# Two feed-forward layers: six interleaved stages a layer instead of three passes, 24 groups of seven products instead of 16

## What is computed

```python
def swiglu(h, w_gate, w_up, w_down):
    return (jax.nn.silu(h @ w_gate) * (h @ w_up)) @ w_down

def reference(x, positions, ...):
    cos, sin = rope_tables(positions)
    for l in range(DEPTH):                       # DEPTH = 2
        if l < N_A:                              # layer 0
            x = x + multiscale_pool_mixer(rms_norm(x, pool_norm[l]), ...)
        else:                                    # layer 1
            x = x + mla_layer_mixer(rms_norm(x, attn_norm[b]), ..., cos, sin)
        x = x + swiglu(rms_norm(x, ffn_norm[l]), w_gate[l], w_up[l], w_down[l])
    return rms_norm(x, final_norm)
```

## Time and profile before

| what | value |
|---|---|
| median of three runs | 1746.03 us |
| the three runs | 1746.16, 1745.45, 1746.03 us |
| the profiled execution | 1746.25 us, its span 1744.4 us |
| PE, DVE, ACT, POOL busy | 1736.1, 1339.1, 986.0, 168.2 us |
| granted PE clock | 1.0 in all slices |
| read from HBM | 326.01 MB |

### The profile page before, as it was taken

One profiled execution on the slowest core, in us unless ns is written; L12 is line 12 of the kernel. 1 busy time (PEld: TensorE's weight loads), 2 busy tenths in 40 slices (PEclk: granted clock), 3 DMA queues, 4 the chain that ended last, 5 costly groups with the idle time before them and its releaser, 6 DMA issues. The chain is left out here.

```text
span 1744.4 us, 29460 instructions
## 1 busy us (share of the span) xinstructions
PE 1736.1 (100%) x11142; PEld 1575.2 (90%) x11142; DVE 1339.1 (77%) x1772; ACT 986.0 (57%) x1336; POOL 168.2 (10%) x196
## 2 busy tenths in 40 slices
PE   9999999999999999999999999999999999999998
PEld 6899988999889999889999888998899998899987
DVE  5898766788667886788997779876678866788665
ACT  6666543566435665466775456664356653466543
POOL 2100000000000000324112420000000000000000
PEclk9999999999999999999999999999999999999999
DMA  6678665786767876665445457867568866688762
GB/s 227 216 231 245 234 192 190 238 252 170 248 200 203 251 232 216 200 199 159 150 139 170 156 165 244 242 186 252 196 191 246 247 214 203 200 252 243 227 214 91
DMA packets 103937, 363.24 MB, mean 208 GB/s; under 512 B 11664, under 2 KB 13072, under 8 KB 103696
## 3 DMA queue, kind: packets, MB, share of 16 engines
q1 hardware_dynamic: 94320, 327.03, 54.5%
q0 software_dynamic: 9216, 33.56, 11.2%
q10 hardware_dynamic: 288, 1.11, 0.2%
HBM read 326.01 MB, written 2.10 MB: 188 GB/s over the span
## 5 line engine op out<-in xcount | busy, mean ns | idle before, releaser
L1594 DVE TENSOR_TENSOR w_lo<-raw,w_hi 128x1024 fp32r<-128x1024 f32 (+1 forms) x720 | 858.0, 1201 | 257.3 <-ACT w_hi L1148 251.4
L1148 ACT ACTIVATE w_hi<-raw 128x1024 fp32r<-128x1024 f32 (+1 forms) x721 | 741.4, 1035 | 473.9 <-PE ps L635 390.2
L634 PE MATMUL ps<-xg,w_hi 128*128 128x512 f32 x1856 | 653.2, 392 | 0.8 <-DVE w_lo L1594 0.3
L635 PE MATMUL ps<-xg,w_lo 128*128 128x256 f32 x1856 | 522.9, 282 | 0.0
L634 PE MATMUL ps<-act,w_hi 128*128 128x512 f32 x1352 | 469.2, 390 | 0.0
L634 PEld LDWEIGHTS ps<-xg,w_hi 128*128 128x128 f32 x1856 | 348.4, 188 | 72.2 <-DVE w_lo L1594 2.3
L635 PE MATMUL ps<-act,w_lo 128*128 128x256 f32 x1352 | 381.2, 282 | 0.0
L635 PEld LDWEIGHTS ps<-xg,w_lo 128*128 128x128 f32 x1856 | 350.4, 189 | 0.0
L634 PEld LDWEIGHTS ps<-act,w_hi 128*128 128x128 f32 x1352 | 253.8, 188 | 53.1
L635 PEld LDWEIGHTS ps<-act,w_lo 128*128 128x128 f32 x1352 | 255.5, 189 | 0.0
L2214 POOL DMA_DIRECT2D raw<-raw x64 | 55.3, 865 | 1128.5 <-DVE raw L1674 977.6
(11 more groups left out here) (232 smaller groups left out, 1961.8 us busy)
## 6 DMA issues: line engine op xcount, KB each, us to landing
raw<-w_plain SPq DMA_DIRECT2D x224, 512.0 KB, 4.6
raw<-w_group SPq DMA_DIRECT2D x128, 512.0 KB, 5.8
raw<-w_down_rest SPq DMA_DIRECT2D x120, 448.0 KB, 4.1
raw<-raw POOLq DMA_DIRECT2D x64, 512.0 KB, 5.7
raw<-w_down_first SPq DMA_DIRECT2D x64, 512.0 KB, 4.4
raw<-w_o SPq DMA_DIRECT2D x32, 512.0 KB, 3.5
raw<-w_q_a SPq DMA_DIRECT2D x8, 512.0 KB, 4.2
raw<-w_kv_a SPq DMA_DIRECT2D x8, 512.0 KB, 4.3
```

The lines of the kernel that those rows point to most:

```text
L634: pe.matmul(ps[:, bank, :], w_hi[:, s, j * P:(j + 1) * P], moving, start=start, stop=False)
L635: return pe.matmul(ps[:, bank, 0:SEQ], w_lo[:, s, j * P:(j + 1) * P], moving[:, 0:SEQ], start=False, stop=stop)
L1148: nc.scalar.activation(dst, src, ACT.Copy).then_inc(hi_ready, 1)
L1594: nc.vector.tensor_tensor(lo, src, hi.bitcast(F32), ALU.subtract).then_inc(lo_ready, 1)
```

## The change

Each layer's 44 tiles are cut into six stages of 8, 6, 6, 8, 8, 8 tiles with 0, 2, 2, 2, 3, 3 groups: 12 groups and 20 plain tiles a layer, where there were 8 groups and 28 plain tiles. One row of 328 chunks a layer takes the place of three up phases and two of the three downs: the 16 down chunks of stage s - 1 (one chunk of six or eight tiles for each d, step "D") are laid among the gate and up chunks of stage s (`evenly(a, b)` spreads the list b evenly among a; "S", "P" and "D" are group, plain and down chunks). Only the last stage's down stands alone behind the row. Groups begin at chunk 20 of a layer, not 24, and the first ones are laid chunk by chunk with the last four plain chunks of stage 0.

Down chunks now go through the three stream slots of `raw`, and have two banks of PSUM for themselves; plain tiles have one pair of banks after stage 0. `act` holds two stages. Parts 0 and 2 of every second group lie in `square` and `root`. A group is turned six chunks after its P4, not four. The 13 rope instructions are single steps at chunks 40, 44, ... 88 of layer 0, with their values in `sin` and `cos`. W11 of the next group is loaded two chunks later in SP's row than before. The token-major end has four chunks, not seven.

```diff
-PASSES = 6
-LAYER_PASSES = PASSES // 2
-PASS_TILES = (16, 14, 14, 16, 14, 14)
-PASS_GROUPS = (2, 3, 3, 2, 3, 3)
-PASS_LEAD = (24, 4, 4, 24, 4, 4)
-PASS_TAIL = 7
+LAYERS = 2
+STAGE_TILES = (8, 6, 6, 8, 8, 8)
+STAGE_GROUPS = (0, 2, 2, 2, 3, 3)
+STAGES = len(STAGE_TILES)
+STAGE_PLAIN = tuple(t - 2 * g for t, g in zip(STAGE_TILES, STAGE_GROUPS))
+LAYER_GROUPS, LAYER_PLAIN = sum(STAGE_GROUPS), sum(STAGE_PLAIN)
+HALF = max(STAGE_TILES)
+GROUPS_FROM = 20
+SETTLE = 8
+ROPE_AT = tuple(range(40, 92, 4))
+TURN_AFTER = 6
+TAIL = 8
+W11_LAG = 5
...
-    groups = PASS_GROUPS[q]
-    seven = [("S", g, r, c) for g in range(groups) for r in PRODUCTS for c in range(2)]
-    plain = [("P", p, c) for p in range(PASS_TILES[q] - 2 * groups) for c in range(4)]
-    lead, tail = PASS_LEAD[q], PASS_TAIL
-    order, mixed, done = plain[:lead], plain[lead:len(plain) - tail], 0
-    for k, s in enumerate(seven):
-        order.append(s)
...
-    return order + plain[len(plain) - tail:]
...
+def up_order():
+
+    seven = [[("S", sum(STAGE_GROUPS[:s]) + g, r, c) for g in range(STAGE_GROUPS[s]) for r in PRODUCTS for c in range(2)]
+             for s in range(STAGES)]
+    plain = [[("P", sum(STAGE_PLAIN[:s]) + p, c) for p in range(STAGE_PLAIN[s]) for c in range(4)] for s in range(STAGES)]
+    early = plain[0][GROUPS_FROM:]
+    order = plain[0][:GROUPS_FROM] + evenly(early, seven[1][:len(early)])
+    seven[1] = seven[1][len(early):]
+    for s in range(1, STAGES):
+        down = [("D", s - 1, d) for d in range(DT)]
+        last = plain[s][-TAIL:] if s == STAGES - 1 else []
+        rest = plain[s][:len(plain[s]) - len(last)]
+        first = min(len(rest), SETTLE // 3)
+        order += evenly(seven[s][:SETTLE - first], rest[:first])
+        order += evenly(seven[s][SETTLE - first:], evenly(down, rest[first:])) + last
+    return order
...
+                    free = freed_by(g - 1, w, c) + (W11_LAG if w == "W11" else 0)
...
+        def plain_bank(p):
+
+            layer, p = divmod(p, LAYER_PLAIN)
+            second = p % 2 if p < STAGE_PLAIN[0] else p == LAYER_PLAIN - 1
+            return (TILE[UPS[layer]] + 2 * second) % 4
+
+        def down_bank(layer, before):
+
+            return (TILE[UPS[layer]] + 2) % 4 + before % 2
...
+        def part_of(g, at):
+
+            if g % 2 and at in (0, 2):
+                return (square if at == 0 else root)[:, :]
+            return part[:, at, :]
...
+            def load_stream(n):
+
+                s, before, e = raw_slot(n), STREAM_NO[n] - STREAM_SLOTS, chunk_elems(n)
                 if before >= 0:
-                    sp.wait_ge(lo_ready, made(PLAIN_AT[before]))
-
...
+            def down_chunk(layer, k):
+
+                _, s, d = UP_ORDER[k]
+                n, before = CHUNK[UPS[layer]] + k, downs_before(layer, k)
+                pe.wait_ge(lo_ready, made(n))
+                if d == 0:
+                    pe.wait_ge(group_ready, layer * LAYER_GROUPS + sum(STAGE_GROUPS[:s + 1]))
+                    pe.wait_ge(act_ready, layer * LAYER_PLAIN + sum(STAGE_PLAIN[:s + 1]))
+                if before >= 2:
+                    pe.wait_ge(down_out, before - 1)
+                for j in range(STAGE_TILES[s]):
+                    mm = product3(n, j, down_bank(layer, before), act[:, act_slot(s, j), :], j == 0, j == STAGE_TILES[s] - 1)
+                mm.then_inc(chunks_used, 1)
...
-                    g = ended(q, k - 4, "P4")
+                    g = ended(layer, k - TURN_AFTER, "P4")
                     if g is not None:
                         turn_parts(g)
...
+                turned_before = g if at == 1 else g - 1
+                if turned_before >= 1:
+                    sc.wait_ge(part_turned, turned_before)
+                nc.scalar.activation(part_of(g, at), src, ACT.Copy).then_inc(part_copied, 1)
...
+                    if layer == 0 and k in ROPE_AT:
+                        rope_step(ROPE_AT.index(k))
...
+            def down_out_of(layer, k, d):
+
+                bank, xd = down_bank(layer, downs_before(layer, k)), x[:, d, :]
+                ve.wait_ge(chunks_used, done_at(layer, k))
+                step(nc.vector.tensor_tensor(xd, ps[:, bank, 0:SEQ], xd, ALU.add))
+                nc.vector.tensor_tensor(xd, ps[:, bank, SEQ:], xd, ALU.add).then_inc(down_out, 1)
...
+                        d = down_ended(at)
+                        if d is not None:
+                            down_out_of(layer, at, d)
...
-                    split(n1 + 2 * d + SPLIT_SLOTS, i)
-                    into_x(t1 + d, d, n1 + 2 * d + 2, i, 4)
-                    if q == LAYER_PASSES - 1:
-                        gained(d, G_ATTN, xg, xg_before + d + 1, i, 4)
-                    split(n1 + 2 * d + 1 + SPLIT_SLOTS, i)
+                for d in range(DT):
+                    into_x(t1 + d, d, n1 + d + 1)
+                    split(n1 + d + SPLIT_SLOTS)
+                    gained(d, G_ATTN, xg, xg_before + d + 1)
```

More of the change, by code:

```diff
@@ L127, with evenly @@
[L127 to L132, removed]
+def evenly(a, b):
+    out, done = [], 0
+    for k, item in enumerate(a):
+        out.append(item)
+        upto = (k + 1) * len(b) // len(a)
+        out += b[done:upto]
+        done = upto
+    return out
@@ L135, in chunk_plan, with stage_of, plain_tile, group_tile @@
+UP_ORDER = up_order()
+UPS = [f"up{layer}" for layer in range(LAYERS)]
+DOWNS = [f"down{layer}" for layer in range(LAYERS)]
+def stage_of(before, k):
+    return next(s for s in range(STAGES) if k < sum(before[:s + 1]))
+def plain_tile(p):
+    s = stage_of(STAGE_PLAIN, p)
+    return s, 2 * STAGE_GROUPS[s] + p - sum(STAGE_PLAIN[:s])
+def group_tile(g):
+    s = stage_of(STAGE_GROUPS, g)
+    return s, 2 * (g - sum(STAGE_GROUPS[:s]))
+def act_slot(s, f):
+    return s % 2 * HALF + f
 def chunk_plan():
@@ L198, in wanted_by, with up_loads @@
     return GROUP_AT[g, {"W11": "P1", "W12": "P1", "W22": "P5", "W21": "P2"}[w], c]
[L201 to L210, removed]
+def up_loads(layer):
+    loads, first = [], CHUNK[UPS[layer]]
+    for k, s in enumerate(UP_ORDER):
+        n = first + k
+        if s[0] != "S":
+            before = STREAM_NO[n] - STREAM_SLOTS
+            free = STREAM_AT[before] if before >= 0 else 0
+            loads.append((max(free, first - 1), n, ("chunk", n)))
+    for g in range(layer * LAYER_GROUPS, (layer + 1) * LAYER_GROUPS):
@@ L649, in bank_free, with long_tile @@
                     pe.wait_ge(evacuated, plus(t - 3, i, per))
-            def long_tile(n, t, operand, kts, i=None, per=0, each=None, product=product3):
-                for c in range(2):
+            def long_tile(n, t, operand, kts, i=None, per=0, each=None, product=product3, first=0, chunks=2):
+                for c in range(chunks):
                     pe.wait_ge(lo_ready, plus(made(n + c), i, BODY))
@@ L1321, in ffn @@
-                with sc.Fori(0, DT // 4 - 1) as i:
-                    for d in range(4):
-                        down(d, i)
-                for d in range(DT - 4, DT):
-                    down(d)
-            ffn(0, 2)
-            sc.wait_ge(angle_ready, 1)
-            nc.scalar.activation(sin[:, :], angle[:, :], ACT.Sin).then_inc(table_ready, 1)
-            nc.scalar.activation(cos[:, :], turns[:, :], ACT.Sin).then_inc(table_ready, 1)
-            ffn(1)
-            ffn(2)
+                n1, t1 = CHUNK[DOWNS[layer]], TILE[DOWNS[layer]]
@@ L1862, in _ @@
+                n1, t1 = CHUNK[DOWNS[layer]], TILE[DOWNS[layer]]
+                for d in range(DT):
+                    into_x(t1 + d, d, n1 + d + 1)
+                    split(n1 + d + SPLIT_SLOTS)
+                    gained(d, G_ATTN, xg, xg_before + d + 1)
+            ffn(0, 2, DT)
             xk_tiles = iter(range(DT))
```

660 lines of the change are left out of this document (330 added, 330 removed).

## The result

The changed kernel takes 1753.86 us, the median of five runs (1753.55 to 1754.66), beside 1745.45 us for the kernel before in five runs: a ratio of 1.0047, 95% interval 1.0033 to 1.0061. It is slower by 8 us, where the prediction said 1746 and no change. The profiled execution took 1753.55 us with a span of 1751.7, against 1746.25 and 1744.4 before.

The account below looks back on a forecast made before the run. PE's own stream of columns was taken to bound the kernel, supplied by DVE's low halves. 1746.25 - 18.1 us won + 18 of new PE waits = 1746, no change within 0.2%; range 1737 to 1757.

Parts of the forecast that it names:

- What bounds the kernel: Whole kernel: time is PE's own stream of columns; DVE, making each chunk's low half, supplies it.
- Fewer columns: PE: eight new groups save 2.0 us each, 16.1 together; 2 us of old waits go; 18.1 us won.
- Dense places: Where group chunks stand close, DVE's work exceeds PE's; with the layer's end, PE waits 8.7 us a layer, some 18 in both.
- The other group starts come out with 0 to 1 us in hand.: Group starts outside the summed dense places: DVE has 0 to 1 us in hand, so no wait was counted.
- rival on late copies: Stage 5: P7's copy and the next W11 come late; at 9.4 us landing 1755, decides from 6 us; chance 0.13.
- Rope steps: Layer 0, chunks 40 to 88: some 0.3 us at the second group; the others lie in room of the seam sums.
- bound of 2 us for held-up copies: Rope steps on SBUF alone might hold up POOL's copies: between nothing and 7 x 0.3 = 2 us; nothing taken.
- The turn takes waits away and costs PE nothing: Turn six chunks behind a group's P4: takes waits away, costs PE nothing, being as long wherever it stands.
- End of a layer: End of a layer's up: the down product needs plain tile 19's activation sooner; PE waits 1.7 us a layer.
- The seams are absorbed: Rival: half of the waits other than the layer's end go, so 1739; with none left 1731.5; chance 0.30.
- DVE does not catch up between seams: Rival, stage 5: idling at down chunks makes DVE set the pace; PE loses 5 us a layer more, 1756; chance 0.15.
- bound of 4 us for the seam sums: Each seam sum may be off by 0.3 to 0.5, ten by 4 us if they err alike: 1741 to 1751.

Follow-up runs that it names:

- e1: Changed kernel with half of each of DVE's quarter sums left out: 1740.86 us, 13.0 below the changed kernel.
- e3: Changed kernel with all work kept and eleven chunks of a layer moved elsewhere in its row by twelve moves: 1735.21 us, 18.7 below the changed kernel.
- e2: Changed kernel without the copies of W11 onto W21, the next W11 loaded after the low half of P6: 1750.92 us, 2.9 less.
- e6: Changed kernel with a group's turn again four chunks behind its P4, not six: 1758.27 us, 4.4 more than the changed kernel.

## Why the prediction was wrong

*What bounds the kernel.* Right. PE's stream sets the time, and DVE's low halves are the supplier that it waits for.

*Fewer columns.* Right within 0.3 us over both terms: 15.3 and 2.5 against 16.1 and 2. A turn costs 0.45, not 0.35: the 0.35 of the earlier trace rows is the time to the next chunk's start, and that chunk then takes 0.1 more. In 24 turns less 16 that is 0.8.

*Dense places.* The way of the sum was right, at every place where it was made: PE waits where it said, and e1 and e3 show that it is DVE's work in that order. Its sizes were short by 0.1 to 0.4 us a layer (the table). Part of that is the 0.1 that each pause costs behind itself, as at a turn, and most of these places have two pauses or more. The 0.2 us that the sum had in stage 5 for the copy that P7 reads shows as no wait. The second group, with its rope step, is the closest: 2.1 a layer and 0.3 more in layer 0, measured 2.2 and 2.5. DVE's low half of chunk 51 ends 164.87 - 150.26 = 14.6 us after it began with the sums of tile 7; the prediction had 14.3 and 0.3:

```profile
150.26 0.69 DVE L1781 TENSOR_TENSOR sums<-ps,cross 128x512 f32<-128x512 f32 x1 [0.71 <-ACT cross L1314]
...
163.73 1.22 DVE L1674 TENSOR_TENSOR w_lo<-raw,w_hi 128x1024 fp32r<-128x1024 f32 x1
164.87 0.29 DVE L1698 TENSOR_SCALAR cos<-sin 128x256 f32<-128x256 f32 x1
```

*"The other group starts come out with 0 to 1 us in hand."* This is the step that failed, with 3.5 us of the 8. It counted DVE's work and PE's at the second group of stage 5 and took the group's data as there. The runs showed DVE idle there for a W11 that landed late, and then behind with its quarter sums: e2 takes the pauses away by the load, e1 most of them by the sums. The rival on late copies had one piece (the next group's W11 waits for the copy), but priced it only for a copy at the worst 9.4 us and set the point from which it decides at a copy of 6. The copies were no slower than before:

```profile
DMA to landing us min/median/max: 4.5/5.4/9.8
```

What neither the sum nor the rival had is the load's own way: its place behind three others in SP's row, and 7.5 us to landing beside the copies where e2 has 6.0. The parts of the lateness, the copies, the place in SP's row and a DVE without its lead at P2, were not separated further. The Trainium skill, page DMA: Bandwidth & Descriptors, section "Anatomy of one DMA — SWDGE (gpsimd) path", gives a transfer a fixed part of about 2.0 us and the rest at 436 GB/s; for 512 KB that would be about 3.2 us, an estimate by that page. The trace does not agree: the copies have 5.4 us from issue to landing in the middle and 4.5 at the least.

*Rope steps.* Right but for one: they cost 0.3 at the second group, as said, and 0.3 at chunk 88 of layer 0, which the prediction had at nothing; neither shows in layer 1. The bound of 2 us for held-up copies was not needed, but it was hardly tried: one rope step met a copy's issue, that at 164.87 of the fence above, and only in the last 0.1 us of an issue that took 0.86 us, as all of them do in the middle. Whether such a step can hold a copy up stays open.

```profile
164.11 0.86 POOL L2301 DMA_DIRECT2D raw<-raw  x1 [1.67 <-DVE raw L1764]
```

*The turn takes waits away and costs PE nothing.* Right, and worth more than was said: 4.4 us by e6.

*End of a layer.* Right: 1.8 us against 1.7, twice. (The old order's room with 14 tiles was 13 x 0.35 = 4.6 us, not over 4.8; it is still more than the 4.1 needed.)

*The rivals.* "The seams are absorbed" is refuted, since every seam that was summed shows its pause. "DVE does not catch up between seams" is refuted by e3. "The copies come late" named the place that was left out, but not its way: P7 waited for no copy, and the copies were at their ordinary time. That 1753.9 lies within 1737 to 1757 is luck in part, since the upper end was held by the prices of two rivals that did not come true. The sum of the forecast was near nothing because a gain of 18 and a loss of 18 stood against each other, so that an error of a third in the loss alone is 0.35% of the time; the bound of 4 us for the seam sums was one for errors that fall alike, and they did, by 2.7, but it had no room for a place left out. The 1.5 us of slightly longer chunks were not priced; why a plain or down chunk behind a group chunk takes 0.01 us more was not tried.

## What to carry to other kernels

When work is laid more densely, price each handover as a chain of its own, not only each engine's work: last reader, copy, the load's place in its queue, the load beside whatever else the DMA engines carry, split, next reader, against what lies between the two on the bound engine. When the supplier is busy for 85 to 90%, its mean load says little: write down, for each place where two bursts of it meet, its row against the other's, and then move one piece of slow work by a few places; twelve such moves gave 18.7 us here without taking any work away. And a gain and a loss of equal size do not make a sure zero: the range is that of their errors.

## What the runs showed of the hardware

A pause costs PE more than its length: the first product behind it takes 0.50 us in the trace where it takes 0.39 otherwise, and the chunk is longer by 0.08 to 0.12 us; the same stands behind each turn. A load of 512 KB lands later beside copies from SBUF onto SBUF: at the second group of stage 5 the same first load took 7.8 us with the two copies on the way and 3.5 without them (e2). Over the whole changed kernel the loads of quarters (SP's line 627) take:

```profile
DMA to landing us min/median/max: 3.5/6.4/9.4
```

SP issues its loads in order: its queue stood still for 19 us at a load that waited for a low half, while 120 GB/s were moved, and its loads then came in a burst of four, with 298 GB/s in the 12 us behind.
